# Second attention of a two-block kernel: scores and maxima two tiles ahead, products with values behind the transposes

## What is computed

```python
q = jnp.concatenate([q[..., :64], apply_rope(q[..., 64:], cos, sin)], axis=-1)   # 16 heads, 96 wide
k = jnp.concatenate([k_nope, jnp.broadcast_to(k_rope, ...)], axis=-1)
for start in range(0, L, 128):
    end = start + 128
    s = jnp.einsum('bqhd,bkhd->bhqk', q[:, start:end], k[:, :end]) * scale
    s = jnp.where(mask[None, None], s, -jnp.inf)          # causal
    p = jax.nn.softmax(s, axis=-1)
    outs.append(jnp.einsum('bhqk,bkhd->bqhd', p, v[:, :end]))
```

## Time and profile before

| what | value |
|---|---|
| median of three runs | 2219.12 us |
| the profiled execution, its own time | 2215.77 us |
| its span | 2213.8 us |
| TensorE busy | 2033.6 us (92%) |
| VectorE busy | 949.4 us (43%) |
| ScalarE busy | 973.7 us (44%) |
| GpSimd busy | 869.4 us (39%) |
| mean granted TensorE clock | 0.961 |

### The profile page before, as it was taken

How to read it: one execution, slowest core, us unless ns; L and a number is a source line. 1 busy time by engine, 2 the same in 40 slices (tenths; PEclk the granted TensorE clock), 3 DMA queues, 4 the chain that set the end, 5 groups by cost and what they waited for, 6 DMA issues and landing times.

```text
span 2213.8 us, 35187 instructions
## 1 busy us (share of the span) xinstructions
PE 2033.6 (92%) x12884; PEld 1797.2 (81%) x12888; DVE 949.4 (43%) x1635; ACT 973.7 (44%) x1622; POOL 869.4 (39%) x506
## 2 busy tenths in 40 slices
PE   8999889997999999979888889999999569999997
PEld 6887668883777778668777889999999459999997
DVE  6874860136333322247577354343300773423102
ACT  3224652325555542244566345455422445545422
POOL 1544214440434444314433144334443644343443
PEclk7999999998999999989999899999999789999998
DMA  9740013330232333212100012322322003232332
GB/s 344 251 157 29 16 44 96 95 95 19 86 95 86 98 100 105 76 42 93 48 0 0 20 49 79 101 85 83 105 89 77 29 29 96 85 98 92 98 103 77
DMA packets 55517, 186.32 MB, mean 84 GB/s; under 512 B 7056, under 2 KB 10384, under 8 KB 55440
## 3 DMA queue, kind: packets, MB, share of 16 engines
q1 hardware_dynamic: 53600, 183.07, 25.6%
q10 hardware_dynamic: 1840, 2.19, 0.3%
HBM read 183.13 MB, written 2.10 MB: 84 GB/s over the span
## 4 chain that ended last, share of the span: by engine, by line
PE 82%; DVE 11%; ACT 3%; issue 2%; POOL 1%; ACTq 0%; DMA 0%; DVEq 0%; POOLq 0%
PE PS L590 68%; PE PS L878 2%; PE PS L653 2%; PE PS L808 2%; PE PS L837 1%; PE PS L764 1%; PE PS L720 1%; PE PS L641 1%; DVE small L2111 1%; POOL X L1258 1%; DVE pool_s L315 1%; PE PS L781 1%; DVE work L2226 1%; DVE work L2287 1%; PE PS L1108 1%
## 5 line engine op out<-in xcount | busy, mean ns | idle before, releaser
L1156 POOL TENSOR_TENSOR w_lo<-w_raw,w_hi 128x1024 fp32r<-128x1024 f32 x281 | 683.0, 2437 | 1027.6 <-ACT w_hi L1336 1027.5
L590 PE MATMUL PS<-H_hi,w_lo 128*128 128x272 f32 (+3 forms) x2152 | 580.1, 321 | 61.9 <-POOL H_lo L1298 25.9
L1336 ACT ACTIVATE w_hi<-w_raw 128x1024 fp32r<-128x1024 f32 (+2 forms) x317 | 309.5, 987 | 739.3 <-PE PS L590 689.0
L590 PE MATMUL PS<-H_lo,w_hi 128*128 128x272 f32 (+3 forms) x2152 | 573.5, 318 | 0.0
L590 PE MATMUL PS<-H_hi,w_hi 128*128 128x272 f32 (+3 forms) x2152 | 573.0, 318 | 0.0
L590 PEld LDWEIGHTS PS<-H_hi,w_lo 128*128 128x128 f32 x2152 | 363.0, 191 | 105.8 <-issue 56.9
L590 PEld LDWEIGHTS PS<-H_lo,w_hi 128*128 128x128 f32 x2152 | 364.2, 192 | 27.0
L590 PEld LDWEIGHTS PS<-H_hi,w_hi 128*128 128x128 f32 x2152 | 363.2, 191 | 27.7
L2226 DVE SCALAR_TENSOR_TENSOR work<-PS,vec,work 128x512 f32<-128x512 f32 (+4 forms) x264 | 187.0, 751 | 462.1 <-ACT work L1641 452.3
L590 PE MATMUL PS<-mid_hi,w_lo 128*128 128x256 f32 (+2 forms) x880 | 222.6, 306 | 3.6 <-DVE work L2226 3.5
L590 PE MATMUL PS<-mid_hi,w_hi 128*128 128x256 f32 (+2 forms) x880 | 221.5, 305 | 0.0
(11 more groups left out here) (273 smaller groups left out, 3031.9 us busy)
## 6 DMA issues: line engine op xcount, KB each, us to landing
w_raw<-stream SPq DMA_DIRECT2D x293, 512.0 KB, 3.6
ada_w<-ada SPq DMA_DIRECT2D x48, 512.0 KB, 6.4
X<-xT SPq DMA_DIRECT2D x8, 256.0 KB, 5.3
yT<-X SPq DMA_DIRECT2D x16, 128.0 KB, 1.7
rel_raw<-rel ACTq DMA_DIRECT2D x4, 256.0 KB, 2.6
vec<-vecs ACTq DMA_DIRECT2D x1, 390.0 KB, 4.0
sin_t<-rope ACTq DMA_DIRECT2D x1, 264.0 KB, 2.8
cos_t<-rope ACTq DMA_DIRECT2D x1, 132.0 KB, 2.6
```

The costliest lines, as they stand in the source:

```text
L590: last = pe.matmul(out[:, c0 + a:c0 + b], w, x[:, a:b], start=start and i == 0, stop=stop and i == 2)
L1156: gp.tensor_tensor(w_lo[:, o], w_raw[:, o], w_hi[:, o].bitcast(F32), ALU.subtract)\
L1336: return act_.activation(out, in_, ACT.Copy, scale=scale)
```

## The change

Three things, all in the queues of PE and DVE of this stage:

1. PE makes the scores of tile t + 2, not t + 1, in step t. They still go to buffer t % 2 after the exponentials of tile t. DVE's maximum moves to t + 2 as well, and behind the low parts of tile t - 1.
2. The products with the values stand behind the transposes of the step.
3. The late call is cut in two: the key blocks 0 to 2 (9 products) at the first tile of the next head, the blocks 3 and 4 (6 products) at its second tile, which alone raises `pv_done`.

```diff
-                def outputs(p, par, late):
+                def outputs(p, par, late, part=None):
...
                     n = nq if late else 2
-                    for j in range(n):
+                    for j in range(n) if part is None else (range(3, n) if part else range(3)):
...
-                    last.then_inc(pv_done, 1)
+                    if part != 0:
+                        last.then_inc(pv_done, 1)
 
                 def step(p, t, first, last):
-                    if t + 1 < U:
-                        scores(p, t + 1)
+                    if t + 2 < U:
+                        scores(p, t + 2)
                     elif not last:
-                        scores(p + 1, 0)
-                    if t % nq == 3:
-                        outputs(p, t // nq, False)
-                    if t == nq + 1:
-                        outputs(p, 0, True)
-                    elif t == 1 and not first:
-                        outputs(p - 1, 1, True)
+                        scores(p + 1, t + 2 - U)
                     turn_over(p, t)
+                    par, i = divmod(t, nq)
+                    if i == 3:
+                        outputs(p, par, False)
+                    elif i < 2 and par:
+                        outputs(p, 0, True, i)
+                    elif i < 2 and not first:
+                        outputs(p - 1, 1, True, i)
 
                 scores(0, 0)
+                scores(0, 1)
                 over_pairs(pe, pairs, U, step)
-                outputs(pairs - 1, 1, True)
+                outputs(pairs - 1, 1, True, 0)
+                outputs(pairs - 1, 1, True, 1)
...
                 def step(p, t, first, last):
                     normalize(p, t)
-                    if t + 1 < U:
-                        maximum(p, t + 1)
-                    elif not last:
-                        maximum(p + 1, 0)
                     if t:
                         weights(p, t - 1)
                     elif not first:
                         weights(p - 1, U - 1)
+                    if t + 2 < U:
+                        maximum(p, t + 2)
+                    elif not last:
+                        maximum(p + 1, t + 2 - U)
                     if t == 2 and not first:
                         take_out(p - 1)
 
                 maximum(0, 0)
+                maximum(0, 1)
```

## The result

The changed kernel took 2193.16 us in the median of four runs (2192.30 to 2194.35) against 2218.53 (2217.37 to 2220.56) for the kernel before: a ratio of 0.9887 with a 95% interval of 0.9874 to 0.9899. It is 25 us faster. The sign was right, the size was not.

The account below looks back on a forecast made before the run. A ring of waits among ACT, PE and DVE, no full engine, bounds the stage. Pace 13.5 us plus 1 for first tiles less 1 for slow clock is 13.5, taken as 14: 2219.1 to 2205 us, range 2196 to 2215.

Parts of the forecast that it names:

- the ring: In the attention stage, ACT, PE and DVE wait on one another in series through PE's queue; no engine is full.
- the pace: Time per half pair between multiplications of fifth tiles: 9.92 us before, forecast 9.0 with the new queues.
- The term of 13.5 us: Gain in the stage's loop: 15 half pairs at 0.9 us each.
- The steps of the layout: New queues with old durations, from DVE's reciprocal of tile 0: low parts done at 1.1 us, tile 4 scores at 5.4.
- the clock's sign: Slow-clock stretches in the stage were to give back time under the new order: 1 us off the gain.
- The layout behind it: Half pair laid out with PE's times doubled: 15.8 us in the new order against 15.3 in the old.
- my second rival: The clock stays up: PE's gaps shrink and 5.8 us come back on top; gain 20, time 2199, chance 0.18.
- PE's share rising from 83% to 90%: Reason given for the clock staying up in the stage: PE's share of busy time rises.
- the first tiles: At the stage's start, work on tiles 1 and 2 runs while the first transposes wait: 1 us gained.
- The lock: Rival: DVE's multiplication of tile 2 also waits for POOL's split through the shared port; gain 6, time 2213, chance 0.12.
- DVE's queue: Rival: DVE's maximum of t + 2 waits for late scores and blocks the next reciprocal; 10 us slower, 2229, chance 0.07.
- The `pv_done` wait: ACT's high parts of a head's third tile wait for later products; 0.9 us a half pair if uncovered, 2219, chance 0.06.

Follow-up runs that it names:

- experiment 2: Changed kernel with the old place and cut of the products, keeping only the two-tile look-ahead: 2196.55 us against 2217.00 for the kernel before.
- experiment 3: Changed kernel with scores and maxima one tile ahead and the maximum first, keeping the moved, cut products: 2227.22 us against 2217.00 for the kernel before.
- experiment 4: Changed kernel with only the six early products of a head back ahead of the transposes: 2189.92 us against 2217.00 for the kernel before.
- experiment 5: Changed kernel with the late products in one piece of 15, behind the transposes: 2203.68 us against 2218.01 for the kernel before.
- experiment 6: Changed kernel with DVE's maximum of two tiles ahead put before the low parts again: 2211.64 us against 2218.01 for the kernel before.
- experiment 7: Changed kernel with all products, both pieces and the early call, ahead of the transposes: 2197.74 us against 2218.01 for the kernel before.
- experiment 1: Kernel before plus 16 small unread products per half pair in PE's gaps, attention's output not the reference's: 2210.98 us against 2217.00 without them.
- experiment 8: Kernel before plus small unread products in PE's gaps, written to clear nothing so every output is computed: 2210.70 us against 2218.01 without them.
- experiment 10: Changed kernel with only the six early products ahead of the transposes: 2190.07 us, beside 2195.35 for the changed kernel on the same chip.
- experiment 11: Changed kernel with early products ahead of the transposes, plus small unread products at both ends of the stage: 2188.65 us, ratio 0.9865 to the kernel before.

## Why the prediction was wrong

**Right: the ring and the pace.** That waits and not an engine paced the stage, and that the new queues give 9.0 us a half pair in place of 9.92. Measured are 8.99, and 8.68 and 9.30 for the halves that I had laid out at 8.9 and 9.5. The term of 13.5 us measured 14.4. The steps of the layout hold too: counted from DVE's reciprocal of tile 0 (1141.89), the low parts are done at 1.1 us as laid out, and DVE can start on the scores of tile 4 at 5.3 (1147.20), where I had 5.4. DVE waits at the maxima of tiles 3 and 4 as said, the transposes wait 7.4 us (I had called 20 wrong), and ACT's wait for the maxima is gone. My layout also told experiments 2 to 6 within 0.2 us a half pair, but not 7.

**Wrong: the clock's sign.** "For the few such stretches I take 1 us off." The half-clock stretches did not stay and cost more; they went, and 5.8 us in the loop and 1.0 behind it came back. That step is 7.8 us (with the 1 us taken off) of the 9.5 between the 14 forecast and the 23.5 of the profiles. The layout behind it, 15.8 against 15.3 us a half at half clock, was never put to the test, since no such half was left. I had the stretches' going as my second rival, with 20 us and 2199, and gave it 0.18. Experiments 1 and 8 show that filling PE's gaps removes the drops, and the price of 6 to 7 us. I gave two reasons for that rival. PE's share rising from 83% to 90% is not the cause: experiment 6 keeps the share of before and has no drop in the loop. The gaps are the other. PE's longest wait between 1088 and 1220 us is 1.2 us in both kernels with drops (before, experiment 3), and 1.0 in experiment 2, 0.8 in 7, 0.7 in 6 and at most 0.6 in 5, 8 and the changed kernel, all without drops between 1092 and 1220 us. That goes with the drops over these runs; it isn't a test of it. And it can't be the whole. The kernel before waits 1.2 us in every second half pair and 1.0 in the others, and the clock falls behind four of the seven waits of 1.2 us and behind one of 1.0. Here is one of 1.2 us behind which it falls and one behind which it doesn't:

```profile
1097.00:1100.00 3.00, 1.59 (x15) 1.23 (x13) 2.38 (x9) 2.32 (x8) 0.00 (x0) 0.93 0.00 0
1100.00:1103.00 3.00, 3.00 (x15) 2.91 (x15) 2.40 (x7) 2.06 (x7) 2.29 (x2) 0.51 0.00 0
...
1160.00:1163.00 3.00, 1.59 (x15) 1.22 (x14) 2.38 (x9) 2.35 (x8) 0.00 (x0) 1.00 0.00 0
1163.00:1166.00 3.00, 3.00 (x25) 2.78 (x25) 2.39 (x7) 2.05 (x7) 2.32 (x2) 1.00 0.00 0
```

So a low stretch like the 1.64 us of the earlier trace rows doesn't foretell a drop by itself, and what else decides stays open. With the clock priced in the main forecast I would have said 2198.

**Too small: the start and the end.** I gave 1 us for the first tiles and it was 1.8, part of it clock; the end of the stage, which I left at nothing without a reason, gave 0.7. With the 0.9 us by which the pace was better this makes another 2.4 us; my rounding of 13.5 up to 14 and 0.3 us ahead of the stage go the other way.

**Rivals.** The lock did not move to a second multiplication in the changed kernel: those of 384 columns stay at 0.42 us from the second head on, and the one of 256 still meets the q split (0.97 to 1.06 us, 0.95 to 1.03 before). But it was close. I had laid that multiplication out 0.4 us behind the end of the k split, and in the rows it starts at most 0.1 us behind it (1146.05 against 1144.66 + 1.30), in all heads but the last two, as it did before the change. In experiments 2, 5 and 7 it meets the split and takes 0.63 to 0.93 us. DVE's queue did not block, because the low parts stand ahead of the maximum; experiment 6 shows that without this the pace is lost. The `pv_done` wait stands at ACT's split of v and not at the high parts, where I looked for it. It is 7.2 us in all in the changed kernel and 21.3 in experiment 5, and in both it is hidden from DVE.

## What to carry to other kernels

Lay the new queues out with the old durations, check the layout on the old order first, and the pace comes out well; but price the clock apart from it, in both directions. If the granted clock falls inside a stage, put work that nothing reads into TensorE's gaps: that measures in one run what the gaps cost in clock, here 6 to 7 us. When an order is changed, look also at what the other engines start beside it: in three of these kernels a multiplication came to start 0.4 to 0.7 us before the end of another engine's split and took 0.2 to 0.5 us longer. Look ahead by the depth of the buffers, but put the operation that waits for the look-ahead behind the one that is already fed.

## What the runs showed that I had not expected

- Sixteen added products a half pair made the kernel 6 to 7 us faster at an unchanged pace of 9.93 us.
- The same mean PE load (109.5 and 110.8 us of 132) goes with full clock in one order of the queues and with a clock of 0.95 in another.
- Behind the stage, where the code is the same, the time moved by 1 us between kernels (963.2 before, 962.1 after), and by 2.1 us more than 70 us behind it between experiments 10 and 11.
- The same wait of PE for 1.2 us, at the same place of the queue, comes seven times in the kernel before; the clock falls behind four of them.
